# Output products of a cross attention by a Strassen scheme with sums in place, and three quarters of their weights loaded twice

## The chip, the cores and the metric

The kernel runs on one core of a Trainium2 chip. The metric is the device time of one execution in microseconds. Of three runs of the kernel before, the median is 2770.35 us (2768.77 to 2773.72).

## The reference, cut to what matters

One layer of a hybrid decoder serves a prompt of 1024 tokens and 64 sample tokens (8 sequences of 8), with a model width of 1024, in float32. This case is about the second of its three residual blocks, the cross attention:

```python
def cross_attn(xn, mem_kv, w_xq, w_xo):
    q = (xn @ w_xq).reshape(B, S, N_XHEADS, XHEAD_DIM)        # 4 heads of 256
    s = jnp.einsum('bqhd,bkhd->bhqk', q, mem_kv[:, :, 0]) * (XHEAD_DIM ** -0.5)
    p = jax.nn.softmax(s, axis=-1)                            # over 256 memory rows
    o = jnp.einsum('bhqk,bkhd->bqhd', p, mem_kv[:, :, 1])
    return o.reshape(B, S, D_MODEL) @ w_xo
...
xp = xp + cross_attn(rmsnorm(xp, g_xattn[l]), mkv, w_xq[l], w_xo[l])
ff, cb = conv_ffn(rmsnorm(xp, g_ffn[l]), ...)
```

The prompt attends to one memory, each of the 8 sample sequences to a cached one of its own. The product with `w_xo` is 1024 x 1024 x 1024 for the prompt and 64 x 1024 x 1024 for the samples.

## The kernel before, in words

Activations stand transposed (128 channels on the partitions, k = 0 to 7 blocks of channels). A matmul takes 128 tokens of one block k as the stationary side and 512 columns of the weights as the moving side. The residual rows `x_res` stay in SBUF, nine tiles: eight of 128 prompt tokens (t = 0 to 7) and one of the 64 samples (t = 8, `NQ`). A float32 matmul stands in the profile as two records on PE.

**The order of work** is written by `weave`. Each stage is a generator on each engine and yields the planned time of its next piece; `weave` always takes the piece with the earliest planned time. Planned times (table `PLAN`, at its end) only sort the instructions of an engine; at this place a planned 1872 stands at about 1751 us of the trace. An engine executes its list in order, and whatever waits holds all that is behind it. Five parts meet around this change:

- **c**, the output products. `onto_x_pe` (L1934 to L1959) runs them for t = 0 to 7 and h = 0, 1 (halves of the output columns): 8 matmuls (L1948) into bank h, 16 units in all, then the samples, 16 matmuls (L1956) that come last. `crossout_dve` adds each unit onto `x_res` from PSUM (L2371, 512 columns an add). Unit u waits until unit u - 2 has been added. Planned 1848 to 2040. `mix_pe`, `mix_sums` and `mix_dve` (L2034 to L2102) are an earlier stage, the output product of the mixer. It has the seven products of the scheme already, 28 prompt units of 4 matmuls (L2049) with four PSUM banks, and the sums of 128x2048 elements (L2062 to L2087).
- **x**, the prompt's attention (`attention`, L651): 16 units x, of which scores are PE L702, the turned probabilities PE L729, the products with the values PE L718, and the copy of these ("taken") DVE L788.
- **xp**, the samples' attention into the cached memories (`paged`, L1212), one batch b = 0 to 7 after the other: four turns of the keys (T, PE L1287; the copies behind them on ACT L1353 and DVE L1346 in turn), scores (S, PE L1303), their copy and maximum (DVE L1378, L1379, L1388), exponential (ACT L1358), turned probabilities (P, PE L1312; copy DVE L1398), product with the values (V, PE L1323; scaled by DVE L1405), and the turn back (O, PE L1330; copies DVE L1409). It begins on each engine with a wait for the last taken unit of x, and has 72 pieces, spread evenly over its planned time (1872 to 2012). The samples' output products wait for its end.
- **n3**, the norm before the MLP, row tile by row tile: square and root on ACT (L325, L328, with an activation table of its own), reciprocal and scaling on DVE (L348, L354), two groups of four turns on PE (L369), and behind each a multiplying copy on DVE (L340). The scaled row has one buffer and the turned one bank. In the planned time of tile i, of length d, the square stands at 0, the scaling at 0.2 d, the turns at 0.5 d and 0.7 d, the copies at 0.6 d and 0.8 d. A tile's planned time was 20.7 us.
- **sums and first products of the MLP**: `token_sums` (DVE L2588 to L2592, three sums a tile, for tiles 4 to 6 between the others, for 7 and 8 behind them), `weight_sums`, and `first_products_pe` (PE L2518), then the turns of the old rows (PE L2474).

SP issues the loads (`cross_sp`, the cached memories L2294 and L2305, the MLP's weights L2465) and `spill_sp` (L2443), which writes finished rows out.

Of the kernel before, what the change touches and what calls it, by code (L numbers as in the profile page):

```python
# [22 lines left out]
P = 128  # L23
# [29 lines left out]
def rows_of(t):  # L53
    return P if t < NQ else SM
# [47 lines left out]
def make_sample_tables():  # L102
# [46 lines left out]
    memkv=(1577, 1636), q=(1650, 1814), x=(1692, 1856), c=(1848, 2040), n3=(1880, 2066), xp=(1872, 2012))  # L149


def at(stage):
# [20 lines left out]
def build(nc, I, O, TAB):  # L173

    with ExitStack() as ctx:
# [1754 lines left out]
        def onto_x(pfx):  # L1930
            s, z = again("onto_x", "w_in0 w_in1 computed added", lambda n: 2 * TT if n in ("computed", "added") else 16)
            return dict(s=s, z=z)

        def onto_x_pe(pe, a, lhs, w, now, ready):  # L1934

            for t in range(NQ):
                for h in range(2):
                    u = 2 * t + h
                    for k in range(KD):
                        yield now((t + 0.5 * h + 0.5 * k / KD) / (NQ + 0.5))  # L1940
                        if k == 0:
                            if h == 0:
                                ready(pe, t)
                            if t == 0:
                                pe.wait_ge(*nth(a, f"w_in{h}", 16))
                            if u >= 2:
                                pe.wait_ge(*nth(a, "added", u - 1))
                        last = pe.matmul(banks[h], lhs(k)[:, t * P:(t + 1) * P], w[h][:, k, :], start=(k == 0), stop=(k == KD - 1))  # L1948
                    last.then_inc(a["s"]["computed"], 1)
            for k in range(KD):  # L1950
                yield now((NQ + 0.5 * k / KD) / (NQ + 0.5))
                if k == 0:
                    ready(pe, NQ)
                    pe.wait_ge(*nth(a, "added", 2 * NQ - 1))
                for h in range(2):
                    last = pe.matmul(banks[0][h * SM:(h + 1) * SM, :], lhs(k)[:, S:TOK], w[h][:, k, :], start=(k == 0),  # L1956
                                     stop=(k == KD - 1))
                    if k == KD - 1:
                        last.then_inc(a["s"]["computed"], 1)  # L1959

        def onto_x_out(t, h):

            return banks[h] if t < NQ else banks[0][h * SM:(h + 1) * SM, :]

        def onto_x_at(t, h):

            return (t + 0.5 * h + 0.5) / (NQ + 0.5) if t < NQ else 1.0 + 0.01 * h
# [170 lines left out]
        xo = onto_x("crossout")  # L2138

        def cross_unit_due(u):  # L2140

# [205 lines left out]
        def xpages_pe(pe):  # L2347
# [2 lines left out]
            yield from pages_pe(pe, pg_x, lambda e, b, i: landed(e, xk_in[b % 2], b // 2 + 1),  # L2350
                                lambda e, b, i: landed(e, xv_in[b % 2], b // 2 + 1))

        def crossout_pe(pe):
            def ready(eng, t):
                if t == 0:
                    eng.wait_ge(cx["copied"], 32)
                if t < NQ:
                    eng.wait_ge(*nth(att_x, "taken", 12 + t // 2 + 1))
                else:
                    pages_over(eng, pg_x)  # L2360
            yield from onto_x_pe(pe, xo, lambda k: oTc[:, k, :], wX, at("c"), ready)

        def crossout_dve(dve):
            now = at("c")
            for t in range(TT):
                r = rows_of(t)
                for h in range(2):
                    yield now(onto_x_at(t, h))
                    dve.wait_ge(*nth(xo, "computed", 2 * t + h + 1))
                    xr = x_res[0:r, t, 512 * h:512 * h + 512]  # L2370
                    dve.tensor_tensor(xr, xr, onto_x_out(t, h), ALU.add).then_inc(xo["s"]["added"], 1)  # L2371


        NH = 14
# [14 lines left out]
        old_rows = take(2 * FF, B2)  # L2389

        def crossout_ready(eng, i):
            eng.wait_ge(*nth(xo, "added", 2 * (i + 1)))

        n3 = norm(all_tiles, lambda i: x_res[0:rows_of(i), i, :], "g_ffn", xnT, 2 * TT + 2,
                  lambda i: take(D, f0 + 15360), 1, take(D, f0 + 10240), banks[2:3], at("n3"), crossout_ready)
        NF2 = 2 * NF
        NU2 = NF2
        NPR = 14
# [39 lines left out]

        def spill_sp(sp):
            for t in range(TT):  # L2440
                yield at("c")((t + 1) / (NQ + 0.5)) + 1
                sp.wait_ge(*nth(xo, "added", 2 * (t + 1)))
                sp.dma_start(rows_out(t), x_res[0:rows_of(t), t, :]).then_inc(s_xrow[group_of_row[t]][0], 16)  # L2443

        def spilled(eng, groups):
# [4 lines left out]
            eng.wait_ge(s_xrow[i][0], s_xrow[i][1] + 32 * len(ROWS_MOVED[i]))  # L2450

        def mlp_sp(sp):
            yield PLAN["xp"][1] + 10
            pages_over(sp, pg_x)
            sp.dma_start(old_rows[0:16, :], I["cache_ffn_conv"][0].rearrange("b i c -> (b i) c")).then_inc(old_in[0], 16)
            for j in range(NF):
                if j == 1:
                    yield PLAN["n3"][1] + 5
                    sp.wait_ge(*nth(n3, "rooted", TT))
                    spilled(sp, WU_ROWS)  # L2460
                if j >= 2:
                    sp.wait_ge(mp["product"], NPR * (j - 1))
                for a in range(2):
                    i, c = 2 * (j % 2) + a, (j + a * NF) * P
                    sp.dma_start(wu[i], w_up[:, :, c:c + P]).then_inc(wu_in[i][0], 16)  # L2465

        def old_rows_pe(pe):
            landed(pe, old_in, 1)
            pe.wait_ge(*nth(xo, "added", 2 * TT))
# [68 lines left out]
        def mlp_act(act):  # L2538
# [8 lines left out]
            act.wait_ge(*nth(xo, "computed", 2 * TT))  # L2547
# [22 lines left out]
        def sums_dve(dve):  # L2570

            for t in range(4, 7):
                yield at("n3")((t + 1.9) / TT)
                dve.wait_ge(*nth(n3, "kept", 2 * (t + 2)))
                token_sums(dve, t)
            yield at("n3")(8.3 / TT)
            weight_sums(dve, 0)
            yield at("n3")(8.35 / TT)
            fourth_sum(dve, 0)

        def token_sums(dve, t):
# [34 lines left out]
        def mlp_dve(dve):  # L2616
# [35 lines left out]
            dve.wait_ge(*nth(xo, "computed", 2 * TT))  # L2652
# [388 lines left out]
        @block.sync  # L3041
        def _(sp):
            start_sp(sp)
            ptab_sp(sp)
            weave(lf_sp(sp), in_turn(*(dilproj_sp(sp, g) for g in range(NG))), gates_sp(sp),
                  foxprep_sp(sp), foxk_sp(sp), dilprep_sp(sp), dilk_sp(sp), dilv_sp(sp),
                  mix_sp(sp), cross_sp(sp), xpages_sp(sp), xvalues_sp(sp), mlp_sp(sp), spill_sp(sp))
            down_sp(sp)

        @block.gpsimd  # L3050
# [81 lines left out]
```

## Time and profile before

| | |
|---|---|
| median of 3 runs | 2770.35 us |
| the profiled execution: its time | 2772.53 us |
| its span | 2770.7 us |
| PE (TensorE matmul) busy | 2728.6 us, 98% |
| DVE (VectorE) busy | 1151.3 us, 42% |
| ACT (ScalarE) busy | 528.3 us, 19% |
| mean granted clock of TensorE | 0.993 |

PE is the matmul engine, PEld its weight loads, DVE VectorE, ACT ScalarE, SPq the DMA queue of SyncE. The chain of waits is followed back from the last instruction. A timeline row gives start and length in us, engine, line, operation, and in brackets how long the engine was idle before it and what ended that. A windows row gives for a stretch the busy us (and instructions) of PE, PEld, DVE, ACT and POOL, then the granted clock (1.00 is 2.4 GHz, 0.50 is 1.2 GHz), the DMA share and GB/s.

### The profile page before, as it was taken

The page shows a single profiled execution, that of the slowest core. Times are in us where ns is not written, and L with a number is a line of the kernel's source. Part 1 is how long each engine was busy: PE and PEld are TensorE (multiplying, and loading weights), DVE is VectorE, ACT ScalarE, POOL GpSimd, SP SyncE. Part 2 cuts the span into 40 slices and gives each one's busy share as a digit, 9 for nine tenths or more (in the row PEclk, how much of TensorE's full clock was granted, in tenths as well). Part 3 has the DMA queues.
Part 4 walks back from the last instruction along what each step waited for, and adds up shares of the span by engine and source line. Part 5 has one row for each costly group of instructions (what it writes and reads, how often), then busy time and mean ns, then how long its engine had stood idle before and what let it go on. Part 6 is the DMA issues. An engine that isn't in the chain of part 4 may idle for free.

```text
span 2770.7 us, 37655 instructions
## 1 busy us (share of the span) xinstructions
PE 2728.6 (98%) x14274; PEld 1857.1 (67%) x14274; DVE 1151.3 (42%) x2788; ACT 528.3 (19%) x1160; POOL 145.4 (5%) x268
## 2 busy tenths in 40 slices
PE   8999999999999999999999999999999999999998
PEld 7655556767655555456644577546888888888887
DVE  2255543332253233333264023345666666654432
ACT  2233323221201112111002112221112112210002
POOL 1000001020101112100000000000000000000000
PEclk9999999999999999999899999999999999999999
DMA  5000102000116778865511400333445433152201
GB/s 189 22 13 9 59 24 65 28 19 20 44 27 198 214 212 262 244 202 171 200 66 61 152 31 31 130 130 115 140 128 172 149 118 125 46 170 91 82 29 65
DMA packets 207160, 294.48 MB, mean 106 GB/s; under 512 B 20781, under 2 KB 145086, under 8 KB 205942
## 3 DMA queue, kind: packets, MB, share of 16 engines
q1 hardware_dynamic: 148150, 187.76, 20.9%
q10 hardware_dynamic: 42976, 89.26, 10.1%
q0 software_dynamic: 15856, 15.07, 2.2%
q8 instruction: 115, 1.88, 0.3%
q14 instruction: 63, 0.52, 0.1%
HBM read 268.07 MB, written 63.35 MB: 120 GB/s over the span
## 4 chain that ended last, share of the span: by engine, by line
PE 96%; DMA 2%; DVE 1%; issue 1%; ACT 0%; SPq 0%; ACTq 0%; DVEq 0%
PE psum L2518 20%; PE psum L955 11%; PE psum L2898 10%; PE psum L1864 9%; PE psum L531 5%; PE psum L2202 4%; PE psum L1948 4%; PE psum L2049 3%; PE psum L702 3%; PE psum L1287 3%; PE psum L718 3%; PE psum L1872 3%; PE psum L1323 3%; PE psum L1303 2%; PE psum L2176 2%; PE psum L729 2%
## 5 line engine op out<-in xcount | busy, mean ns | idle before, releaser
L2518 PE MATMUL psum<-arena 128*128 128x272 f32 x2464 | 567.3, 394 | 0.5 <-DVE arena L2592 0.5
L2518 PEld LDWEIGHTS psum<-arena 128*128 128x128 f32 x2464 | 470.2, 191 | 97.0 <-issue 0.6
L955 PE MATMUL psum<-arena 128*128 128x512 f32 (+3 forms) x960 | 316.9, 481 | 1.4 <-ACT arena L584 1.4
L1864 PE MATMUL psum<-arena 128*128 128x368 f32 (+1 forms) x768 | 298.2, 489 | 1.4 <-DVE arena L1807 1.2
L2898 PE MATMUL psum<-arena 128*128 128x256 f32 (+1 forms) x1584 | 288.1, 356 | 0.0
L2898 PEld LDWEIGHTS psum<-arena 128*128 128x128 f32 (+1 forms) x1584 | 252.8, 178 | 34.3 <-issue 3.2
L955 PEld LDWEIGHTS psum<-arena 128*128 128x128 f32 (+1 forms) x960 | 195.1, 250 | 62.3 <-issue 35.1
L778 DVE CUSTOM_DVE_ANT_0 arena<-psum,arena 128x256 f32<-128x256 f32 (+2 forms) x224 | 95.4, 457 | 207.0 <-PE psum L702 206.6
L1864 PEld LDWEIGHTS psum<-arena 128*128 128x128 f32 x768 | 123.2, 190 | 68.2 <-issue 42.1
L2621 DVE TENSOR_TENSOR arena<-arena,psum 128x272 f32<-128x272 f32 (+2 forms) x330 | 111.7, 377 | 112.8 <-PE psum L2518 112.0
L752 ACT ACTIVATE arena<-arena 128x256 f32<-128x256 f32 (+4 forms) x192 | 107.5, 562 | 228.7 <-DVE arena L778 227.2
L1287 PEld LDWEIGHTS psum<-arena 128*128 128x128 f32 x848 | 102.1, 141 | 66.4 <-issue 42.1
L1346 DVE COPY arena<-psum 128x512 f32<-128x512 f32 (+1 forms) x108 | 73.6, 682 | 166.2 <-PE psum L1287 166.2
L531 PE MATMUL psum<-arena 128*128 128x288 f32 (+1 forms) x384 | 137.6, 483 | 0.0
L1353 ACT ACTIVATE arena<-psum 128x512 f32<-128x512 f32 (+1 forms) x108 | 63.6, 589 | 377.8 <-PE psum L1287 357.3
L2642 DVE SCALAR_TENSOR_TENSOR arena<-arena 128x1024 f32<-128x1024 f32 x88 | 113.1, 1285 | 52.6 <-ACT arena L2544 51.1
L1287 PE MATMUL psum<-arena 128*128 128x128 f32 x848 | 130.2, 276 | 3.9 <-DMA arena<-in_cache_fox_kv 3.7
L2542 ACT ACTIVATE arena<-arena 128x1024 f32<-128x1024 f32 x44 | 54.2, 1233 | 400.7 <-DVE arena L2621 400.7
L1948 PE MATMUL psum<-arena 128*128 128x512 f32 x256 | 123.5, 599 | 0.0
L2202 PE MATMUL psum<-arena 128*128 128x288 f32 (+1 forms) x384 | 122.6, 468 | 0.0
L3001 DVE TENSOR_TENSOR arena<-arena,psum 128x256 f32<-128x256 f32 (+1 forms) x128 | 46.6, 401 | 178.9 <-PE psum L2898 178.8
L788 DVE COPY arena<-psum 128x128 f32<-128x128 f32 (+1 forms) x96 | 37.6, 391 | 193.4 <-PE psum L718 193.2
(242 smaller groups left out, 2973.7 us busy)
## 6 DMA issues: line engine op xcount, KB each, us to landing
arena<-in_cache_fox_kv ACTq DMA_DIRECT2D x128, 256.0 KB, 4.3
arena<-in_cache_fox_kv SPq DMA_DIRECT2D x128, 256.0 KB, 4.4
out_win_s<-in_cache_win_kv ACTq DMA_DIRECT2D x8, 4080.0 KB, 15.4
arena<-in_w_up SPq DMA_DIRECT2D x44, 512.0 KB, 6.3
arena<-in_w_down SPq DMA_DIRECT2D x14, 1408.0 KB, 6.3
arena<-in_cache_win_kv SPq DMA_DIRECT2D x16, 1024.0 KB, 7.9
arena<-in_cache_mem_kv SPq DMA_DIRECT2D x16, 1024.0 KB, 6.3
arena<-in_w_in SPq DMA_DIRECT2D x9, 1024.0 KB, 7.8
```

The lines of the kernel that those rows point to most:

```text
L531: last = pe.matmul(banks[q % 2][:, 0:cw], w[:, k, j * P:(j + 1) * P], xnT[:, k, c0:c0 + cw], start=(k == 0), stop=(k == KD - 1))
L752: act.activation(p, p, ACT.Exp, scale=-1.0, bias=a["NM"][i], accum_out=a["L"][i]).then_inc(s["expd"], 1)
L778: dve.tensor_tensor_reduce(a["Pb"][i % 4][:, c0:c1], SCORE[h][:, 0:c1 - c0], un["add"](h)[:, c0:c1], 1.0, a["GM"][:, i % 4:i % 4 + 1] if c ...
L955: last = pe.matmul(banks[c0 // 512][p0:p0 + r, 0:n], xn_tile(k, g, t), wD[g][:, k, w0:w0 + n], start=(k == 0), stop=(k == KD - 1))
L1287: last = pe.transpose(a["turn"][n % 2][:, x * P:(x + 1) * P], k, ident)
L1864: last = pe.matmul(banks[0][:, 0:cw], w[:, k, :], xnT[:, k, c0:c0 + cw], start=(k == 0), stop=(k == KD - 1))
L1948: last = pe.matmul(banks[h], lhs(k)[:, t * P:(t + 1) * P], w[h][:, k, :], start=(k == 0), stop=(k == KD - 1))
L2202: last = pe.matmul(banks[u % 2][:, 0:cw], wX[n % 2][:, k, (m % 4) * P:(m % 4 + 1) * P], xnT[:, k, c0:c0 + cw], start=(k == 0), stop=(k == ...
L2518: last = pe.matmul(bank_of(j, x, p), w[:, k, :], r[:, k, Q4 * p:Q4 * p + Q4], start=(k == 0), stop=(k == 3))
L2621: last = dve.tensor_tensor(dst, dst if base is None else view(base), view(bank), ALU.add)
L2642: dve.scalar_tensor_tensor(out=tp, in0=up[:, tap:tap + S], scalar=w, in1=tp, op0=ALU.mult, op1=ALU.add).then_inc(done, 1)
L2898: last = pe.matmul(down_out(u)[p0:p0 + r, 0:n], hT(f)[:, tok + t * P:tok + t * P + r], slot[slots[c]][:, f - fa, c0:c0 + n], start=(f == f ...
```

## The change

The prompt's output products are cut into quarters (512 tokens, 512 channels, 512 columns) and computed by seven products in place of eight. There are 28 units of 4 matmuls in two banks, four for each product, then the samples' unit of 16 matmuls. The quarter sums are formed in place: four over the attention's output, four over the weights. For the samples, whose output needs the plain weights, three quarters of `w_xo` are loaded again, each when its last reader is done. Rows 0 to 3 of `x_res` are now complete with product p6 and rows 4 to 7 with p4, the last. The planned times of c, xp and n3 are new, and so is the point where the samples' products stand (2032).

```diff
-    ... c=(1848, 2040), n3=(1880, 2066), xp=(1872, 2012))
+    ... c=(1844, 2004), n3=(1972, 2066), xp=(1872, 2024))
-            yield from onto_x_pe(pe, xo, lambda k: oTc[:, k, :], wX, at("c"), ready)
+        C_UNITS = [(name, t) for name in ("p1", "p2", "p7", "p5", "p3", "p6", "p4") for t in range(4)] + [("s", NQ)]
+        N_CU = len(C_UNITS)
+        def cross_at(u):
+            return at("c")(u / 28) if u < 28 else 2032 + 10 * (u - 28)
+        def cross_over(u):
+            return at("c")((u + 1) / 28) if u < 28 else 2042
+        def n3_at(x):
+            return 1972 + 5.7 * 9 * x if 9 * x < 8 else 2043 + 23 * (9 * x - 8)
+        def cross_again_sp(sp):
+            yield cross_over(c_done("p7") - 1) + 1
+            sp.wait_ge(*nth(xo, "computed", c_done("p7")))
+            sp.dma_start(wX[1][:, 0:4, :], w_xo[:, 0:4, 512:1024]).then_inc(xo["s"]["w_in1"], 16)
+            yield cross_over(c_done("p6") - 1) + 1
+            sp.wait_ge(*nth(xo, "computed", c_done("p6")))
+            sp.wait_ge(*nth(cw, "summed", 4))
+            sp.dma_start(wX[0][:, 0:4, :], w_xo[:, 0:4, 0:512]).then_inc(xo["s"]["w_in0"], 16)
+            yield cross_over(c_done("p4") - 1) + 1
+            sp.wait_ge(*nth(xo, "computed", c_done("p4")))
+            sp.dma_start(wX[0][:, 4:8, :], w_xo[:, 4:8, 0:512]).then_inc(xo["s"]["w_in0"], 16)
+        def cross_operands_ready(pe, name):
...
+            elif name == "p7":
+                pe.wait_ge(*nth(cw, "summed", 2))
+                pe.wait_ge(*nth(ch, "summed", 1))
...
+            else:
+                pages_over(pe, pg_x)
+                pe.wait_ge(*nth(xo, "w_in1", 32))
+                pe.wait_ge(*nth(xo, "w_in0", 48))
         def crossout_pe(pe):
+            for u, (name, t) in enumerate(C_UNITS):
+                yield cross_at(u)
+                if t == 0 or name == "s":
+                    cross_operands_ready(pe, name)
+                if u >= 2:
+                    pe.wait_ge(*nth(xo, "added", u - 1))
...
+                    for k in range(4):
+                        if k:
+                            yield cross_at(u + k / 4)
+                        last = pe.matmul(banks[u % 2], oTc[:, ks, tok + t * P:tok + (t + 1) * P][:, k, :], wX[side][:, ws, :][:, k, :],
+                                         start=(k == 0), stop=(k == 3))
+                last.then_inc(xo["s"]["computed"], 1)
+        def cross_sums(dve, name, t):
+            if (name, t) == ("p2", 0):
+                dve.wait_ge(*nth(xo, "computed", c_done("p1")))
+                dve.wait_ge(*nth(att_x, "taken", 8))
+                dve.tensor_tensor(part(M_LOW, 0), part(M_LOW, 0), part(M_LOW, 512), ALU.subtract).then_inc(ch["s"]["summed"], 1)
+                dve.wait_ge(*nth(xo, "w_in0", 16))
+                dve.wait_ge(*nth(xo, "w_in1", 16))
+                dve.tensor_tensor(b11, b12, b11, ALU.subtract).then_inc(cw["s"]["summed"], 1)
+            elif (name, t) == ("p2", 1):
...
         def crossout_dve(dve):
+            for u, (name, t) in enumerate(C_UNITS):
+                yield cross_over(u)
+                dve.wait_ge(*nth(xo, "computed", u + 1))
+                for half, side in M_ONTO.get(name, ((2, 0), (2, 1))):
...
+                    last = dve.tensor_tensor(xr, xr, src, ALU.add)
+                last.then_inc(xo["s"]["added"], 1)
+                cross_sums(dve, name, t)
+        def cross_row_done(i):
+            return N_CU if i == NQ else c_done("p6", i) if i < 4 else c_done("p4", i - 4)
 def spill_sp(sp):
-                yield at("c")((t + 1) / (NQ + 0.5)) + 1
+                yield cross_over(cross_row_done(t) - 1) + 2
 def mlp_sp(sp):
-            yield PLAN["xp"][1] + 10
+            yield PLAN["xp"][1] + 4
 def first_products_pe(pe):
-                    yield at("c")(1.02) + 0.1 * (2 * x + p)
+                    yield 2043.8 + 0.1 * (2 * x + p)
 def sums_dve(dve):
-                yield at("n3")((t + 1.9) / TT)
+                yield n3_at((t + 1.9) / TT)
```

The other sums follow the pattern shown: one behind the adds of (p2, 1), (p7, 0), (p5, 0), (p5, 1), (p3, 0) and (p3, 1). An add of a unit of p1 has four parts (one for each quarter of the output), p2, p3 and p4 one, p7 and p5 two, p6 three. The three reloads are of 1 MB each.

## Rows read from the trace of the kernel before

**Rows 1.** The page: busy time of the engines, and the chain's shares

```profile
PE 2728.6 (98%) x14274; PEld 1857.1 (67%) x14274; DVE 1151.3 (42%) x2788; ACT 528.3 (19%) x1160; POOL 145.4 (5%) x268
PE 96%; DMA 2%; DVE 1%; issue 1%; ACT 0%; SPq 0%; ACTq 0%; DVEq 0%
```

**Rows 2.** Window over most of the stage

```profile
1752.00:1877.00 125.00, 125.00 (x658) 61.36 (x657) 48.49 (x120) 40.58 (x66) 0.00 (x0) 1.00 0.42 148
```

**Rows 3.** Groups by line, 1729 to 1910 us: busy, mean ns, idle before

```profile
L1948 PE MATMUL psum<-arena 128*128 128x512 f32 x256 | 123.5, 599 | 0.0
L2371 DVE TENSOR_TENSOR arena<-arena,psum 128x512 f32<-128x512 f32 (+1 forms) x18 | 12.3, 684 | 16.3 <-PE psum L1948 14.2 <-PE psum L1956 2.0
```

**Rows 4.** Timeline of DVE in the mixer's output product

```profile
1411.56 2.28 DVE L2062 TENSOR_TENSOR arena<-arena 128x2048 f32<-128x2048 f32 x1
1413.76 2.29 DVE L2066 TENSOR_TENSOR arena<-arena 128x2048 f32<-128x2048 f32 x1
...
1469.32 1.89 DVE L2099 SCALAR_TENSOR_TENSOR arena<-psum,arena 128x512 f32<-128x512 f32 x3 [1.55 <-PE psum L2049]
...
1472.75 1.89 DVE L2099 SCALAR_TENSOR_TENSOR arena<-psum,arena 128x512 f32<-128x512 f32 x3 [0.69 <-PE psum L2049]
```

**Rows 5.** Timeline of PE where the prompt's attention ends

```profile
1750.52 1.02 PE L1948 MATMUL psum<-arena 128*128 128x512 f32 x2
1751.67 0.63 PE L1287 MATMUL psum<-arena 128*128 128x128 f32 x4
```

**Rows 6.** Timeline of ACT: an exponential, then a row of the norm

```profile
1775.88 0.51 ACT L1358 ACTIVATE arena<-arena 128x256 f32<-128x256 f32 x1 [2.25 <-DVE arena L1388]
...
1776.38 1.04 ACT L325 ACTIVATE arena<-arena 128x1024 f32<-128x1024 f32 x1
...
1777.54 1.28 ACT L328 ACT_TABLE_LOAD   x1
1778.83 0.29 ACT L328 ACTIVATE arena<-arena 128x1 f32<-128x1 f32 x1
```

**Rows 7.** Timeline of DVE, 1859 to 1885 us

```profile
1865.05 0.48 DVE L1405 TENSOR_SCALAR arena<-psum,arena 128x256 f32<-128x256 f32 x1 [2.37 <-issue]
...
1868.76 0.42 DVE L1378 COPY arena<-psum 128x256 f32<-128x256 f32 x1 [0.58 <-PE psum L1303]
...
1869.43 0.55 DVE L2588 TENSOR_TENSOR arena<-arena 128x384 f32<-128x384 f32 x1
...
1876.29 0.75 DVE L354 TENSOR_SCALAR arena<-arena 128x1024 f32<-128x1024 f32 x1
...
1882.81 0.69 DVE L340 TENSOR_TENSOR arena<-psum,arena 128x512 f32<-128x512 f32 x1 [0.61 <-PE psum L369]
1883.53 0.69 DVE L2588 TENSOR_TENSOR arena<-arena 128x512 f32<-128x512 f32 x1
```

**Rows 8.** Timeline of PE, 1866 to 1910 us

```profile
1866.69 1.02 PE L1948 MATMUL psum<-arena 128*128 128x512 f32 x2
1867.64 1.05 PE L1303 MATMUL psum<-arena 128*8 128x256 f32 x16
1868.63 2.84 PE L1948 MATMUL psum<-arena 128*128 128x512 f32 x6
...
1876.36 0.38 PE L1330 MATMUL psum<-arena 128*128 128x128 f32 x2
...
1888.71 4.51 PE L1956 MATMUL psum<-arena 128*64 128x512 f32 x20
...
1909.87 20.36 PE L2518 MATMUL psum<-arena 128*128 128x272 f32 x78 [0.54 <-DVE arena L2592]
```

**Rows 9.** Where the clock fell: a row of PE's timeline, two windows

```profile
1397.45 1.09 PE L369 MATMUL psum<-arena 128*128 128x128 f32 x8 [2.43 <-DVE arena L354]
1366.00:1370.00 4.00, 4.00 (x21) 4.00 (x20) 0.00 (x0) 0.00 (x0) 0.00 (x0) 0.50 1.05 395
1400.00:1404.00 4.00, 4.00 (x14) 1.10 (x12) 0.30 (x1) 0.00 (x0) 0.00 (x0) 0.70 0.00 0
```

More of the change, by code:

```diff
@@ L1927, in gates_dve @@
             dve.tensor_tensor(merged[:, :, S:TOK], sgs[:, 0, :, :], sgs[:, 1, :, :], ALU.add).then_inc(gt["s_merged"], 1)
[L1930 to L1967, printed above, removed]
         wm = [take(4096, f0 + 4096 * i).rearrange("p (k n) -> p k n", k=KD) for i in range(2)]
@@ L2351, in xpages_pe @@
                                 lambda e, b, i: landed(e, xv_in[b % 2], b // 2 + 1))
-        def crossout_pe(pe):
[L2354 to L2358, printed above, removed]
-                else:
-                    pages_over(eng, pg_x)
-            yield from onto_x_pe(pe, xo, lambda k: oTc[:, k, :], wX, at("c"), ready)
-        def crossout_dve(dve):
[L2364 to L2371, printed above, removed]
+        def cross_operands_ready(pe, name):
+            if name == "p1":
+                pe.wait_ge(cx["copied"], 32)
+                pe.wait_ge(*nth(att_x, "taken", 8))
+                pe.wait_ge(*nth(xo, "w_in0", 16))
+            elif name == "p2":
+                pe.wait_ge(*nth(att_x, "taken", 14))
+            elif name == "p7":
+                pe.wait_ge(*nth(cw, "summed", 2))
+                pe.wait_ge(*nth(ch, "summed", 1))
+            elif name == "p5":
+                pe.wait_ge(*nth(ch, "summed", 2))
+            elif name == "p3":
+                pe.wait_ge(*nth(ch, "summed", 4))
+            elif name == "p6":
+                pe.wait_ge(*nth(cw, "summed", 3))
+            elif name == "p4":
+                pe.wait_ge(*nth(cw, "summed", 4))
+            else:
+                pages_over(pe, pg_x)
+                pe.wait_ge(*nth(xo, "w_in1", 32))
+                pe.wait_ge(*nth(xo, "w_in0", 48))
@@ new lines, in crossout_pe @@
+        def crossout_pe(pe):
+            for u, (name, t) in enumerate(C_UNITS):
[4 more added lines that the diff above has]
+                    pe.wait_ge(*nth(xo, "added", u - 1))
+                if name == "s":
+                    for k in range(KD):
+                        if k:
+                            yield cross_at(u + k / KD)
+                        for h in range(2):
+                            last = pe.matmul(banks[u % 2][h * SM:(h + 1) * SM, :], oTc[:, k, S:TOK], wX[h][:, k, :],
+                                             start=(k == 0), stop=(k == KD - 1))
+                else:
+                    ks, tok, side, ws = M_WHERE[name]
+                    for k in range(4):
+                        if k:
+                            yield cross_at(u + k / 4)
+                        last = pe.matmul(banks[u % 2], oTc[:, ks, tok + t * P:tok + (t + 1) * P][:, k, :], wX[side][:, ws, :][:, k, :],
+                                         start=(k == 0), stop=(k == 3))
+                last.then_inc(xo["s"]["computed"], 1)
@@ new lines, in cross_sums, with part @@
+        def cross_sums(dve, name, t):
+            def part(ks, tok):
+                return oTc[:, ks, tok:tok + 512]
+            b11, b21, b12, b22 = wX[0][:, M_LOW, :], wX[0][:, M_HIGH, :], wX[1][:, M_LOW, :], wX[1][:, M_HIGH, :]
+            if (name, t) == ("p2", 0):
[6 more added lines that the diff above has]
+            elif (name, t) == ("p2", 1):
+                dve.wait_ge(*nth(cw, "summed", 1))
+                dve.tensor_tensor(b12, b22, b12, ALU.subtract).then_inc(cw["s"]["summed"], 1)
+            elif (name, t) == ("p7", 0):
+                dve.wait_ge(*nth(ch, "summed", 1))
+                dve.wait_ge(*nth(att_x, "taken", 16))
+                dve.tensor_tensor(part(M_LOW, 512), part(M_LOW, 512), part(M_HIGH, 512), ALU.add).then_inc(ch["s"]["summed"], 1)
+            elif (name, t) == ("p5", 0):
+                dve.wait_ge(*nth(xo, "computed", c_done("p7")))
+                dve.wait_ge(*nth(ch, "summed", 2))
+                dve.tensor_tensor(part(M_LOW, 0), part(M_HIGH, 512), part(M_LOW, 0), ALU.subtract).then_inc(ch["s"]["summed"], 1)
+            elif (name, t) == ("p5", 1):
+                dve.wait_ge(*nth(xo, "computed", c_done("p2")))
+                dve.wait_ge(*nth(ch, "summed", 3))
+                dve.tensor_tensor(part(M_HIGH, 0), part(M_HIGH, 0), part(M_LOW, 0), ALU.subtract).then_inc(ch["s"]["summed"], 1)
+            elif (name, t) == ("p3", 0):
+                dve.wait_ge(*nth(xo, "computed", c_done("p5")))
+                dve.wait_ge(*nth(cw, "summed", 2))
+                dve.tensor_tensor(b11, b22, b11, ALU.subtract).then_inc(cw["s"]["summed"], 1)
+            elif (name, t) == ("p3", 1):
+                dve.wait_ge(*nth(cw, "summed", 3))
+                dve.tensor_tensor(b21, b21, b11, ALU.subtract).then_inc(cw["s"]["summed"], 1)
@@ new lines, in crossout_dve @@
+        def crossout_dve(dve):
+            for u, (name, t) in enumerate(C_UNITS):
+                yield cross_over(u)
+                dve.wait_ge(*nth(xo, "computed", u + 1))
+                for half, side in M_ONTO.get(name, ((2, 0), (2, 1))):
+                    tile_, r = (4 * half + t, P) if half < 2 else (NQ, SM)
+                    xr = x_res[0:r, tile_, 512 * side:512 * side + 512]
+                    src = banks[u % 2] if half < 2 else banks[u % 2][side * SM:(side + 1) * SM, :]
+                    last = dve.tensor_tensor(xr, xr, src, ALU.add)
+                last.then_inc(xo["s"]["added"], 1)
+                cross_sums(dve, name, t)
@@ L2391, in crossout_ready @@
         def crossout_ready(eng, i):
-            eng.wait_ge(*nth(xo, "added", 2 * (i + 1)))
+            eng.wait_ge(*nth(xo, "added", cross_row_done(i)))
         n3 = norm(all_tiles, lambda i: x_res[0:rows_of(i), i, :], "g_ffn", xnT, 2 * TT + 2,
-                  lambda i: take(D, f0 + 15360), 1, take(D, f0 + 10240), banks[2:3], at("n3"), crossout_ready)
+                  lambda i: take(D, f0 + 15360), 1, take(D, f0 + 10240), banks[2:3], n3_at, crossout_ready)
         NF2 = 2 * NF
@@ L2440, in spill_sp @@
             for t in range(TT):
-                yield at("c")((t + 1) / (NQ + 0.5)) + 1
-                sp.wait_ge(*nth(xo, "added", 2 * (t + 1)))
+                yield cross_over(cross_row_done(t) - 1) + 2
+                sp.wait_ge(*nth(xo, "added", cross_row_done(t)))
                 sp.dma_start(rows_out(t), x_res[0:rows_of(t), t, :]).then_inc(s_xrow[group_of_row[t]][0], 16)
@@ L2468, in old_rows_pe @@
             landed(pe, old_in, 1)
-            pe.wait_ge(*nth(xo, "added", 2 * TT))
+            pe.wait_ge(*nth(xo, "added", N_CU))
             for q in range(2):
@@ L2651, in mlp_dve @@
             dve.wait_ge(mp["old_turned"], 1)
-            dve.wait_ge(*nth(xo, "computed", 2 * TT))
+            dve.wait_ge(*nth(xo, "computed", N_CU))
             dve.wait_ge(*nth(n3, "turned", 2 * TT))
```

18 lines of the change are left out of this document (12 added, 6 removed).

## The prediction

> **What bounds the kernel now.** I read the page first: PE is busy for 98% of the span and carries 96% of the chain that ended last [rows 1]. The reader should see that a microsecond taken from PE's list is gained only while PE stays fed. The window over the stage says it is: 125.00 of 125 us busy, with DVE at 39% and ACT at 32% [rows 2]. The groups by line give the size: the prompt's output products are 256 records with no idle time before them [rows 3]. The timelines then show what holds the stage so full. The prompt's attention hands over to the samples' pages with no gap worth naming [rows 5], and single matmuls of the output product stand between all small pieces of the pages [rows 8]. They are the filler that hides every chain through DVE and ACT. The last page piece starts at 1876.36, and 12 us of products still follow before the samples' unit at 1888.71 [rows 8].
>
> **What is removed.** In the mixer's stage, a prompt unit of four matmuls takes 1472.75 - 1469.32 = 3.43 us, 0.86 a matmul [rows 4]. Eight products become seven: 128 matmuls become 112, so PE's list is shorter by 16 x 0.86 = **13.7 us**. The samples' unit is the same.
>
> **What is added off PE.** DVE gets 56 adds for 16, 40 x 0.6 = 24 us (three in a row take 1.89 [rows 4]), and eight sums of 2.2 = 18 us [rows 4]. In a stage of some 165 us it goes from about 39% to about 65%: no bound by its total. With two banks a unit's adds must be over before the second next unit starts, 3.4 us later and more: the longest, four adds, take 2.5 and fit. I cost the bank ring at nothing; if DVE comes late once, it is under 1 us. The three reloads are issued by SP with 0.4 us each. Two have tens of microseconds, the last has all of the tail below (21 us); an 8 us landing is covered by it. They would show only if the tail went.
>
> **What the new order exposes.** I wrote out the lists of PE, DVE and ACT from the planned times and went through them with the durations of the rows. An instruction starts when its engine is free and what it waits for is done, plus 0.05 us. The same working on the old order ends at 1909.9 us, where the trace has 1909.87 [rows 8].
>
> *Where the pages begin: 4.2 us.* The add of (p2, 0) is planned at 1872.57 and the last taken unit at 1872.91, so DVE does the add and two sums first: 0.6 + 2.2 + 2.2, then 0.7 for the copy, 5.8 us after the unit's last matmul. PE has only the 1.7 us of that attention unit's product with the values, and then the first turn of the pages, which waits for the copy. Before, two records of the output product stood there and hid it [rows 5]. 5.8 + 0.2 - 1.7 gives 4.2.
>
> *Row 1 of the norm: 3.2 us.* A norm row now has 5.7 planned us, its first turn 2.85 after its square. On ACT the square of row 1 stands behind the exponential of batch 5. From the start of that batch's scores on PE: scores 1.2, until DVE has done three other adds, the copy, the maximum and a keep 3.2, exponential 0.6, square to root 2.7 with the table load [rows 6], reciprocal and scaling 0.95 [rows 7], 7.6 in all. PE has scores, a turn, three matmuls and O, 4.4 us. Other small stops of the stretch come to 1.6 us.
>
> *The tail: 13.3 us.* The products are planned to end at 2004, the pages at 2024. Behind the last product PE has P and V of batch 6, two turns, S, P, V and O of batch 7, O of 6, and the turns of norm rows 5, 6 and 7: 2 x 0.22, 2 x 0.44, 3 x 1.2 (1.05 and the gaps beside it [rows 8]), 2 x 0.22 and 6 x 0.44, 7.9 us, and no matmul between them. DVE has to do between them three groups of token sums (1.8, 2.2 and 2.2 us: three of 0.55, then of 0.69 [rows 7]), two scalings with reciprocal (0.95), six copies of 0.6 to 0.7, and the pages' copies. In order, PE idles 0.95 us for the copy between the turns of row 5; 2.4 for row 6's scaling, behind the token sums of tile 4; 1.6 for its copy, behind a key copy; 3.5 for row 7's scaling, behind the token sums of tile 5 and the scores' copy of 0.67 [rows 7]; 0.7 for its copy; 3.2 for batch 7's V, whose P copy stands behind the token sums of tile 6; 0.55 for O behind the scaling of 0.48 [rows 7]; 0.55 for the samples' unit. Sum 13.35. What follows that unit (first products, row 8) is as before.
>
> *The clock.* After an idle of 2.43 us among turns the granted clock fell for part of the next window (0.70 over 4 us), and in a stretch of stops and narrow products it stayed at 0.50, 1.2 GHz [rows 9]. The new tail is such a stretch. Nothing shows how long it lasts here. Lower end: 0. Upper end: from 8 us into the tail to the middle of the first products, with PE's pieces on the path twice as long, 7.6, and a spell of 3.4 us costing 1.7 at each of the two stalls ahead, 11 in all. I take 4.1, one spell over the tail's last two thirds and the samples' first half, nearest to the row of 0.50.
>
> Sum: -13.7 + 4.2 + 3.2 + 1.6 + 13.3 - 0.2 (stops of the old order that go) = **+8.4**, with the clock +12.5. The profiled execution, 2772.53 us (span 2770.7), would become 2785; on the median, 2.2 below it, **2783 us**. What a measurement of this kernel can tell from no change is about 0.2%, 5.5 us.
>
> **A rule against the change.** The Trainium skill (TensorE: Matmul & The Clock Gate, "A second HAM failure mode") says that frequent short idles between groups of matmuls, without one long gap, are enough for the clock to swing between half and full. Here row and rule agree in direction [rows 9]; by the rule the upper end of the clock's cost would be the one to take. The sums above do not need it.
>
> **Rivals.**
> 1. *The clock stays down from the first stalls through the samples' unit and the first products.* For it: the 0.50 window above. Against it: the stretch up to the tail is dense. 8.4 + 11 = +19.4, 2790 us.
> 2. *The stalls are half of what I count*, because a wait is met earlier on ACT or DVE (rooted rows ahead, copies overlapping). Then 11 of 22 us stay and the clock holds: -13.7 + 11 + 2 = about -1 to +5, 2769 to 2775, same.
> 3. *The other side: faster.* One mechanism: PE is fed in the tail after all, because the pages' chain and the norm are done by the time the products end. It decides where the last product's end and the end of batch 7 meet. If PE idles there under 3 us and only the 4.2 at the pages' start stays, -13.7 + 4.2 + 3 = -6.5, down to -12 with both gone: 2758 to 2764. For it: before, pages and norm never made PE wait in this stage [rows 2]. Against it: planned 20 us of pages stand behind the last product, and PE's list has no filler there. With the tail gone the last reload would show too.
> 4. *The change doesn't do what it says*: a reload lands so late that the samples' unit waits for it. It would take over 21 us; together with a DVE that falls behind the two banks, above 2793.
>
> **How the numbers follow.** My forecast (2777 to 2787) has 0.52, rival 1 0.18, rival 2 0.16, rival 3 0.10, rival 4 0.04. The range leaves out rivals 3 and 4 and the bottom of rival 2: 2771 to 2793. Same is 2764.8 to 2775.9: rival 2 nearly whole, 0.15. Faster: rival 3, 0.10. Slower: the rest, 0.75.
>
> **What the profile would show.** Right: L1948's groups replaced by 224 records; PE idle of about 4 us released by DVE's taken copy where the pages begin; one of about 3 us before a turn of the norm, released by the scaling; a window of some 21 us before the samples' unit with PE busy for 8 to 12; clock under 1.00 there; the MLP after it unchanged but later. Wrong: that window full, or idle time before the prompt units released by their adds, or by a DMA at the samples' unit. PE's busy time should fall by 10 to 13 us while the span grows.

## The result, and the profile after

The changed kernel takes 2788.48 us (median of 4 runs, 2785.87 to 2791.83) against 2771.81 us of the kernel before (4 runs; the 2770.35 above is the median of the first three): ratio 1.006, 95% interval 1.0042 to 1.0079. It is slower by 16.7 us. The profiled execution took 2786.17 us with a span of 2784.4, so its own difference is 13.7 us of span.

The page of the changed kernel, the lines that answer to [rows 1]:

```profile
PE 2719.7 (98%) x14242; PEld 1845.9 (66%) x14242; DVE 1192.8 (43%) x2836; ACT 520.4 (19%) x1154; POOL 145.4 (5%) x268
PE 94%; DMA 2%; DVE 2%; issue 1%; ACT 0%; ACTq 0%; SPq 0%; DVEq 0%
```

PE is busy for 8.9 us less and the span is 13.7 us longer. DVE is busy for 41.5 us more. PE's share of the chain falls from 96% to 94%. The groups by line over the stage, 1729 to 1925 us, answer to [rows 3]. L2392 are now the prompt's output products, L2385 the samples', and L2440 their adds on DVE:

```profile
L2392 PE MATMUL psum<-arena 128*128 128x512 f32 x220 | 109.1, 612 | 0.0
L2440 DVE TENSOR_TENSOR arena<-arena,psum 128x512 f32<-128x512 f32 (+1 forms) x58 | 37.2, 681 | 19.7 <-PE psum L2392 9.8 <-PE psum L2385 9.8
L369 PE MATMUL psum<-arena 128*128 128x128 f32 (+1 forms) x72 | 12.9, 308 | 11.8 <-DVE arena L354 8.8 <-DVE arena L340 3.0
```

The prompt's products never wait (0.0), so the two banks and their adds cost nothing. The costliest waits are those before the norm's turns, 11.8 us. Timeline rows of PE that have an idle time before them, from the pages' start to the samples' unit:

```profile
1754.56 1.09 PE L1287 MATMUL psum<-arena 128*128 128x128 f32 x4 [4.26 <-DVE arena L788]
...
1852.84 1.11 PE L369 MATMUL psum<-arena 128*128 128x128 f32 x4 [2.94 <-DVE arena L354]
...
1866.71 0.66 PE L369 MATMUL psum<-arena 128*128 128x128 f32 x4 [0.78 <-DVE arena L354]
...
1879.31 0.66 PE L369 MATMUL psum<-arena 128*128 128x128 f32 x4 [0.79 <-DVE arena L340]
...
1883.78 0.65 PE L369 MATMUL psum<-arena 128*128 128x128 f32 x4 [2.40 <-DVE arena L354]
...
1886.25 0.98 PE L369 MATMUL psum<-arena 128*128 128x128 f32 x4 [1.38 <-DVE arena L340]
...
1891.71 1.11 PE L369 MATMUL psum<-arena 128*128 128x128 f32 x4 [2.66 <-DVE arena L354]
...
1893.61 1.11 PE L369 MATMUL psum<-arena 128*128 128x128 f32 x4 [0.36 <-DVE arena L340]
...
1897.93 1.89 PE L1323 MATMUL psum<-arena 128*8 128x256 f32 x16 [2.78 <-issue]
...
1900.48 0.69 PE L1330 MATMUL psum<-arena 128*128 128x128 f32 x2 [0.66 <-DVE arena L1405]
...
1901.56 9.73 PE L2385 MATMUL psum<-arena 128*64 128x512 f32 x32 [0.38 <-DVE arena L1409]
```

They sum to 19.4 us. In the kernel before this stretch has no idle row of this kind [rows 2]. The lengths show the clock as well: four turns take 0.66 us at full clock and 1.11 at half, the samples' unit 9.73 us where it took 7.3 in the kernel before. Windows of the changed kernel (busy us of PE, PEld, DVE, ACT, POOL, then granted clock, DMA share, GB/s), before, in and behind the waits:

```profile
1753.00:1757.00 4.00, 2.44 (x6) 1.58 (x7) 1.30 (x2) 0.60 (x1) 0.00 (x0) 0.54 0.34 81
1757.00:1761.00 4.00, 4.00 (x11) 2.11 (x10) 0.69 (x1) 0.00 (x0) 0.00 (x0) 0.61 0.98 358
1765.00:1850.00 85.00, 84.77 (x424) 39.32 (x422) 49.17 (x93) 14.79 (x29) 0.00 (x0) 1.00 0.47 164
1853.00:1857.00 4.00, 4.00 (x16) 2.57 (x17) 2.82 (x5) 0.17 (x1) 0.00 (x0) 0.66 0.41 156
1886.00:1907.00 21.00, 13.91 (x64) 5.78 (x66) 9.14 (x22) 0.60 (x2) 0.00 (x0) 0.51 0.24 38
```

Between the two places PE is full (84.77 of 85 us). At each of the three places the clock falls to 1.2 GHz, and from 1886 to 1907 us it is at 0.51.

**A length that leaves the rest out.** Single runs of one kernel differ by up to 19 us (22 runs of the kernel before: 2762.64 to 2781.82), and the stretch before this stage alone moved by up to 19 us between traces. So the experiments are also read by one length inside the trace: from the start of the first product with `w_xq` to the start of the last product with `w_up`. Everything the change touches lies in it. The views by line of the kernel before and of the changed one (min, median and max ns; first and last start in us):

```profile
L2202 PE MATMUL psum<-arena x384: 405/407/595, 1555.8 to 1715.4; 128*128 128x288 f32 x128, 128*128 128x512 f32 x64
L2518 PE MATMUL psum<-arena x2464: 392/393/792, 1897.0 to 2469.3; 128*128 128x272 f32 x190
```

```profile
L2198 PE MATMUL psum<-arena x384: 406/406/595, 1552.8 to 1712.4; 128*128 128x288 f32 x128, 128*128 128x512 f32 x64
L2593 PE MATMUL psum<-arena x2464: 392/392/792, 1911.2 to 2483.0; 128*128 128x272 f32 x190
```

Before: 2469.3 - 1555.8 = 913.5 us. After: 930.2 us, **16.7 us** more, which is the difference of the medians too. The stretch ahead, which the change does not touch, was 3 us shorter in this trace; in another trace of the same order of work (e4 below) it is 4 us longer.

### The profile page after: what moved, and what is told of

Read it like the earlier page. It is cut to its first block, busy times and chain, and to the rows that moved or that the text cites. A ratio compares the mean times of both kernels' runs of the same rounds, so it can differ in the third digit from the quotient of the medians.

```text
span 2784.4 us, 37643 instructions
## 1 busy us (share of the span) xinstructions
PE 2719.7 (98%) x14242; PEld 1845.9 (66%) x14242; DVE 1192.8 (43%) x2836; ACT 520.4 (19%) x1154; POOL 145.4 (5%) x268
## 4 chain that ended last, share of the span: by engine, by line
PE 94%; DMA 2%; DVE 2%; issue 1%; ACT 0%; ACTq 0%; SPq 0%; DVEq 0%
PE psum L2593 20%; PE psum L955 11%; PE psum L2973 10%; PE psum L1864 9%; PE psum L531 5%; PE psum L2198 4%; PE psum L1287 3%; PE psum L702 3%; PE psum L2392 3%; PE psum L1872 3%; PE psum L718 3%; PE psum L2010 3%; PE psum L1323 2%; PE psum L1303 2%; PE psum L2172 2%; PE psum L729 2%
## 5 line engine op out<-in xcount | busy, mean ns | idle before, releaser
L788 DVE COPY arena<-psum 128x128 f32<-128x128 f32 (+1 forms) x96 | 37.5, 391 | 184.8 <-PE psum L718 184.6
L2392 PE MATMUL psum<-arena 128*128 128x512 f32 x224 | 110.9, 612 | 0.0
```

What stands on the lines that cost most here:

```text
L2392: last = pe.matmul(banks[u % 2], oTc[:, ks, tok + t * P:tok + (t + 1) * P][:, k, :], wX[side][:, ws, :][:, k, :], start=(k == 0), stop=(k ...
```

## The experiments

Theory: PE's list is 13.7 us shorter, and the new order opens waits at three places where nothing fills PE, in which the clock falls. Rivals: the pages or the norm bound the stage anyway; DVE's added work; the reloads; or only waits and no clock. Eight experiments were made. The times of e1 to e4 are set against 22 runs of the kernel before (median 2769.09 us), those of e5 to e8 against 35 (2772.80).

A stage length is that of one execution. To each belong two more figures, taken over the same stretch of the same trace: the time in which PE is idle, and the time in which PE is busy while the granted clock is at 0.50. The last column adds up three terms against the kernel before: the list of PE (-13.8 us, as e2 measures it; e3 adds the 15.4 us of its fillers), the difference in idle time, and half of the difference in busy time at 0.50. The half is an estimate: it takes the work to be twice as long at half clock.

| run | stage length, us | against before | ratio of times to before, 95% interval | PE idle, us | PE busy at 0.50, us | sum of the three terms |
|---|---|---|---|---|---|---|
| before | 913.5 | | | 1.7 | 6.3 |  |
| changed | 930.2 | +16.7 | 1.006 (1.0042 to 1.0079) | 21.8 | 25.3 | +15.8 |
| e1_changed_again | 930.2 | +16.7 | 1.0052 (1.0033 to 1.0072) | 21.8 | 25.4 | +15.9 |
| e2_before_112 | 899.7 | -13.8 | 0.9962 (0.9945 to 0.9979) | 1.7 | 6.3 | -13.8 |
| e3_filled_stalls | 922.5 | +9.0 | 1.0031 (1.0017 to 1.0044) | 8.4 | 5.9 | +8.1 |
| e4_small_reloads | 931.8 | +18.3 | 1.0072 (1.005 to 1.0095) | 21.8 | 29.0 | +17.7 |
| e5_sums_later | 923.4 | +9.9 | 1.0031 (1.0016 to 1.0045) | 18.6 | 17.9 | +8.9 |
| e6_token_sums_later | 928.4 | +14.9 | 1.0039 (1.0022 to 1.0056) | 18.4 | 28.8 | +14.2 |
| e7_pages_earlier | 921.8 | +8.3 | 1.0017 (1.0006 to 1.0029) | 16.7 | 16.6 | +6.4 |
| e8_all_reordered | 903.8 | -9.7 | 0.9972 (0.9958 to 0.9986) | 5.9 | 3.3 | -11.1 |

The sum comes within 2 us of every length, so PE's list, its idle time and the half clock are nearly all that the runs differ by. By the whole times e3, e5 and e6 are not told apart from the changed kernel (their intervals overlap that of e1); what they show rests on the lengths and the traces.

**The changed kernel once more.**

> The changed kernel once more, beside the kernel before, for the size of the loss and its spread. My theory (stalls of PE at three places where its list has no filler, and the clock that falls in them): 12 to 18 us slower, ratio 1.0045 to 1.0065. If the loss shown so far were a matter of which runs were taken (rival: no change), under 5 us.

Measured: 14.8 us slower (2783.91 against 2769.09), stage length 930.2 again, with the waits of 4.26, 2.94, 2.40, 2.67 and 2.78 us in the same places. The waits are set by the order, not by chance.

**The shorter list alone, in the old order.**

```diff
 def onto_x_pe(...)
-                    for k in range(KD):
+                    for k in range(KD - 1):
...
-                                    start=(k == 0), stop=(k == KD - 1))
+                                    start=(k == 0), stop=(k == KD - 2))
```

> The kernel before with the last of the eight channel blocks left out of the prompt's output products: 112 matmuls in place of 128, as in the scheme, and nothing else moved. This is the shorter list of PE alone. Theory: every microsecond less on PE is gained while PE stays fed, so 13.7 us faster, ratio 0.995; PE idle time in the stage under 3 us. Rival: the pages or the norm are the true bound of the stage and hold the end where it was: under 5 us gained, and PE idles before turns.

Measured: the length is 13.8 us shorter, the time 7.7 us by the medians, 10.5 by the ratio. This kernel leaves out one block of channels, so its result is wrong. The windows of this kernel over the stage:

```profile
1752.00:1862.00 110.00, 109.87 (x581) 55.98 (x579) 42.68 (x105) 37.86 (x61) 0.00 (x0) 1.00 0.47 163
1862.00:1890.00 28.00, 28.00 (x136) 12.06 (x136) 12.95 (x29) 4.77 (x9) 0.00 (x0) 1.00 0.37 88
```

PE stays fed with 112 matmuls in the old order. The rival (pages or norm as the true bound) falls: 16 matmuls less are worth their 0.86 us each.

**Idle time filled with matmuls that nobody reads.**

```diff
+        def filler_pe(pe):
+            for due, n, b, done in ((1871.95, 8, 1, 4), (1980.5, 6, 0, 23), (2009.0, 5, 0, 27), (2010.1, 2, 0, 27),
+                                    (2014.7, 6, 0, 27), (2019.7, 6, 0, 27)):
+                yield due
+                pe.wait_ge(*nth(xo, "added", done))
+                for _ in range(n):
+                    pe.matmul(banks[b][:, 0:256], ident, cst["band_mask"], start=True, stop=True)
```

> The changed kernel with 33 matmuls of 128x256 that nobody reads put into PE's list just before the places where it waits (8 where the pages begin, 6 before the first turn of norm row 1, 19 in the tail): some 14 us of idle time filled, and none of the waits changed. If the clock is a part of the loss, as the 0.50 windows say, the granted clock of the tail rises to 1.00 and the time falls by 3 to 8 us against the changed kernel. If only the waits count (rival), the time stays or grows by up to 3 us, since some fillers are longer than what is left of a wait.

Measured: the length falls by 7.7 us against the changed kernel, at the upper end of what was expected, and the medians by 6.4 (2777.56 against 2783.91). Windows of the filled tail, to be held against 1886 to 1907 above:

```profile
1880.00:1900.00 20.00, 16.72 (x123) 11.29 (x122) 13.92 (x31) 5.14 (x10) 0.00 (x0) 1.00 0.20 76
1900.00:1910.00 10.00, 10.00 (x47) 4.93 (x44) 1.37 (x2) 1.95 (x3) 0.00 (x0) 1.00 0.83 160
```

The clock is at 1.00 in the tail and at both stalls ahead of it, and the samples' unit takes 7.09 us. More work on PE made the stage shorter. The fillers are 15.4 us of work where PE's idle time fell by 13.4, so some 2 us of them outlast the waits. What is left, +9.0, is near the +8.4 that the prediction has for the waits without the clock.

**The second loads without their bytes.**

```diff
-            sp.dma_start(wX[1][:, 0:4, :], w_xo[:, 0:4, 512:1024])...
+            sp.dma_start(wX[1][0:1, 0:4, :], w_xo[0:1, 0:4, 512:1024])...
...
```

(and so for the other two loads)

> The changed kernel with the three second loads of the weights cut from 1 MB to one partition's part of it, so that the samples' products take wrong weights for three quarters. Same number of loads and waits, almost no bytes. Theory: the reloads lie under the tail, so no change against the changed kernel (within 3 us). Rival (the second loads delay the pages' loads, or the samples' unit waits for them): 4 to 10 us faster than the changed kernel.

Measured: nothing gained; the length is 1.6 us longer than that of the changed kernel, with the same waits, and the clock was low for 6.8 us in place of 3.4 both at the second stall and where the MLP begins. The median is 7.3 us above that of e1 (2791.21 against 2783.91), more than the 3 us expected, but the intervals of the two ratios overlap, and of the 7.2 us between the two profiled spans the stage length has only 1.6. In the changed kernel the last reload landed 4.9 us after its issue, some 19 us before the samples' unit began. The rival falls.

**The sums where the pages begin, moved behind the copy.**

```diff
             if (name, t) == ("p2", 0):
+                yield 1873.0
                 dve.wait_ge(*nth(xo, "computed", c_done("p1")))
...
+                yield 1880.0
                 dve.wait_ge(*nth(xo, "w_in0", 16))
...
-                cross_sums(dve, name, t)
+                yield from cross_sums(dve, name, t)
```

> The changed kernel with one thing moved on DVE: the first sum over the attention's output comes at a planned 1873.0, behind the copy of the last taken unit (1872.91), and the first sum over the weights at 1880.0. Theory: PE's wait of 4.26 us where the pages begin shrinks to about 1 us, another of about 1 us appears behind the sums, and the clock does not fall there: 3.6 us of waits and 3.4 us of clock less than the changed kernel, stage from the first q product to the last MLP product near 924 us (930.2 in the changed kernel). Rival: the wait only moves to the next piece that needs DVE, nothing gained (930).

Measured: 6.8 us less length (923.4, 924 expected). DVE's timeline in the changed kernel, then in this one:

```profile
1748.61 0.69 DVE L2440 TENSOR_TENSOR arena<-arena,psum 128x512 f32<-128x512 f32 x1 [0.95 <-PE psum L2392]
1749.22 2.28 DVE L2405 TENSOR_TENSOR arena<-arena 128x2048 f32<-128x2048 f32 x1
1751.42 2.29 DVE L2408 TENSOR_TENSOR arena<-arena 128x2048 f32<-128x2048 f32 x1
1753.62 0.68 DVE L788 COPY arena<-psum 128x512 f32<-128x512 f32 x1
```

```profile
1753.25 0.69 DVE L2442 TENSOR_TENSOR arena<-arena,psum 128x512 f32<-128x512 f32 x1 [0.95 <-PE psum L2392]
1754.97 0.69 DVE L788 COPY arena<-psum 128x512 f32<-128x512 f32 x1 [1.04 <-PE psum L718]
1755.85 2.29 DVE L2406 TENSOR_TENSOR arena<-arena 128x2048 f32<-128x2048 f32 x1 [0.19 <-DVE arena L788]
```

Two sums stood between an add and the copy (L788) that lets the pages begin. With the sums behind it PE waits 0.98 us for 4.26, and the clock holds there. The expected wait of 1 us behind the sums didn't come. In the tail the low clock lasted as long as before (6.8 and 13.7 us in two spells). At row 1 of the norm PE still waits 2.94 us, but here the clock held, which was not expected:

```profile
1849.00:1856.00 7.00, 4.74 (x22) 2.75 (x23) 5.12 (x14) 2.54 (x5) 0.00 (x0) 1.00 0.60 215
```

So the gain is some 3.2 us of waits and some 3.7 us of clock, and the clock's part comes from two places, not from the pages' start alone. Whether moving the sums kept the clock up at row 1 or chance did is not shown.

**The token sums, moved behind the pages.**

```diff
-                yield n3_at((t + 1.9) / TT)
+                yield 2030 + t
```

> The changed kernel with the token sums of tiles 4 to 6 (6.2 us of DVE) moved behind the last piece of the pages. Theory: they stand on DVE in front of what PE waits for in the tail, so the tail's idle time falls from 13.3 to 9 us, and the stage by 4.3 us and up to 2 of clock, to 924 to 926 us. Rival: what PE waits for is the chain of the pages itself, not DVE's queue, and the sums were in its gaps: under 1.5 us gained.

Measured: 1.8 us less, where 4.3 to 6 were expected. The three waits of the tail did shrink, from 2.40, 2.66 and 2.78 to 2.06, 1.74 and 0.59 us, 3.5 together. But this trace has a spell of 6.8 us of low clock at the norm's row 1 where the changed one has 3.4, and 17.1 in the tail and 6.8 at the MLP's start for 20.5 and 3.4. PE is busy at 0.50 for 3.5 us more in all, which costs half of it: 3.4 us less of idle time and 1.7 us more of slower work give the 1.8 us. So the token sums are a part of the tail's waits, and the smaller one.

**The pages, planned to end at 2011.**

```diff
-    ... xp=(1872, 2024))
+    ... xp=(1872, 2011))
```

> The changed kernel with the pages planned to end at 2011 in place of 2024, so that fewer of them stand behind the last product. Theory: the matmuls of p4 stand between them again, 5.9 us of waits less, and with the clock 6 to 12 less: stage 918 to 924 us. PE still waits for the scaling of row 7 (4 us). Rival: DVE, with 13 us less for the same adds, sums and copies, makes PE wait earlier in the stage, before the units or before the pages' pieces: no gain (928 to 932).

Measured: 8.4 us less (921.8, 918 to 924 expected). The wait at row 1 of the norm is gone, that at the end of the pages is 0.80 us, and the wait for row 7's scaling grew to 3.82 us, as expected. DVE did not make PE wait before a unit; one wait of 0.64 us appeared before a page's P.

**Everything reordered.**

```diff
-    ... c=(1844, 2004), n3=(1972, 2066), xp=(1872, 2024))
+    ... c=(1844, 2006), n3=(1972, 2066), xp=(1872, 2011))
...
-            return at("c")(u / 28) if u < 28 else 2032 + 10 * (u - 28)
+            return at("c")(u / 28) if u < 28 else 2014.5 + 10 * (u - 28)
...
-            return 1972 + 5.7 * 9 * x if 9 * x < 8 else 2043 + 23 * (9 * x - 8)
+            i = int(9 * x + 1e-6)
+            return 1972 + 5.7 * i + 7.2 * (9 * x - i) if i < 8 else 2025.5 + 23 * (9 * x - 8)
...
             if (name, t) == ("p2", 0):
+                yield 1877.5
                 dve.wait_ge(*nth(xo, "computed", c_done("p1")))
...
+                yield 1878.0
                 dve.wait_ge(*nth(xo, "w_in0", 16))
...
-                yield n3_at((t + 1.9) / TT)
+                yield 2012 + t
-                    yield 2043.8 + 0.1 * (2 * x + p)
+                    yield 2026.3 + 0.1 * (2 * x + p)
```

(`cross_over` of the samples' unit moves with `cross_at`, from 2042 to 2024.5)

> All three together, and the samples' unit, the first products and the norm's row 8 moved up by 17.5 planned us, with row 7's turns inside the samples' unit; within a norm row the scaling and turns come 26% later behind its square, and c ends at 2006. Theory: the waits fall from 23 to about 6 us and the clock holds outside the end, so that the 13.7 us of products are kept for the most part: stage 903 to 907 us, 7 to 10 us under the kernel before, ratio 0.9965. The last reload is the next thing to wait for (1.6 us). Rival: some wait that the order hid so far (the reload, DVE behind the two banks) takes back what is gained, and the stage ends no better than before (913 us or more).

Measured: 903.8 us, 26.4 less than the changed kernel and 9.7 less than the kernel before; 2765.89 against 2772.80 us, ratio 0.9972 (0.9958 to 0.9986). It beats both, though its gain over the kernel before is 4.1 us short of what the list is worth (13.8); PE is idle for 5.9 us over the stage length, for 1.7 before. Windows over the stage, and the idle rows of its end:

```profile
1752.00:1877.00 125.00, 124.47 (x646) 61.56 (x644) 81.96 (x153) 29.95 (x58) 0.00 (x0) 1.00 0.47 165
1877.00:1885.00 8.00, 5.30 (x40) 2.22 (x38) 6.47 (x15) 1.60 (x4) 0.00 (x0) 1.00 0.91 244
```

```profile
1878.78 0.44 PE L1330 MATMUL psum<-arena 128*128 128x128 f32 x2 [0.67 <-DVE arena L1405]
1879.63 0.66 PE L369 MATMUL psum<-arena 128*128 128x128 f32 x4 [0.42 <-DVE arena L354]
1881.08 0.66 PE L369 MATMUL psum<-arena 128*128 128x128 f32 x4 [0.79 <-DVE arena L340]
1882.56 1.08 PE L2386 MATMUL psum<-arena 128*64 128x512 f32 x4 [0.83 <-DMA arena<-in_w_xo]
```

DVE is at 82 of 125 us there, 66%, and holds PE up once, for 0.40 us before a turn of the norm. The reload is the next wait, as expected, with 0.83 us.

## Why the prediction was right

It said 2783 us, slower with a chance of 0.75. Measured were 2788.5, inside the range (2771 to 2793), 5.5 us above the forecast and 1.5 us above the likeliest case's own range (2777 to 2787). The path was right: the list of PE shorter by what was said, and waits opened at the three places named. Two terms were off in opposite directions. The waits came to 20.1 us for 22.1, the clock to 10.4 for 4.1; that the first error took a third of the second back is luck.

- *The term removed*: 13.7 us forecast, 13.8 measured alone (e2).
- *Where the pages begin*: 4.2 us forecast, 4.26 in the trace, released by DVE's L788. e5 shows the two sums as the cause. The terms written there give 4.3 (5.8 + 0.2 - 1.7), not 4.2.
- *Row 1 of the norm*: 3.2 forecast, 2.94 in the trace. The *other small stops* ahead of the tail came to 0.78 us for 1.6.
- *The tail*: the eight waits were forecast as 0.95, 2.4, 1.6, 3.5, 0.7, 3.2, 0.55, 0.55. They came as 0.79, 2.40, 1.38, 2.66, 0.36, 2.78, 0.66, 0.38: 11.4 us for 13.45, as the eight terms add up (13.35 is a slip, as is 7.9 for PE's own work there, which adds up to 8.0). The 21 us before the samples' unit, 1880.5 to 1901.5, have PE busy for 10.44, where 8 to 12 were forecast. Part of the difference is PE's own work at half clock, which fills the waits it lies beside (turns of 1.11 us, a V of 1.89). That this is a cause is argued, not shown.
- *DVE's total, the banks and the reloads at nothing*: right. PE waits for no unit's add and for no load, and DVE's busy time grew by 41.5 us where 42 were forecast. PE's busy time fell by 8.9 us and not by 10 to 13, since work at half clock is busy for longer.
- *The clock*: the term that was mis-sized. The prediction took 4.1 us, one spell over two thirds of the tail and half of the samples' unit, and left the two stalls ahead to its upper end. The trace has a spell at each stall (6.8 and 3.4 us) and one of 20.5 us, over the last 15 us of the tail and the first half of the samples' unit. What the waits leave of the 16.7 is this: PE is idle for 21.8 us over the stage length and for 1.7 before, so 16.7 + 13.8 - 20.1 = 10.4 us are slower work, near the prediction's upper end of 11. Two other readings agree. Half of the busy time at 0.50, 25.3 us against 6.3 before, is 9.5 us. And e3, in which no spell is left ahead of the MLP, gives back 7.7 us although some 2 us of its fillers outlast the waits. The kernel before has a spell of its own where the MLP begins (6.8 us, 3.4 in the changed kernel), which the prediction did not count. For its row of 0.50 the prediction speaks of stops and narrow products; PE was busy for 4.00 of 4 us in that row [rows 9], so it is a row of narrow work rather than of stops.

The first rival had more of this mechanism than the forecast, with 2790 us for its price, and the measured time lies nearer to it. But its "stays down from the first stalls" is not what happened: between the stalls and the tail the clock was at 1.00, for 85 us from 1765 to 1850, and only 3.4 us of the first products ran at half.

The Trainium skill's rule that frequent short idles let the clock swing (TensorE: Matmul & The Clock Gate, "A second HAM failure mode") spoke for that rival. The Trainium skill tells it there of another kernel, in bf16. This trace agrees that no long wait is needed: 0.51 over 1886 to 1907 us, with no idle over 2.8 us in it. It differs in that the clock did not swing there but stayed at half for 20.5 us. The rival on the other side, that PE would be fed in the tail, fell with the rows above; the order of e8 makes it true, at its price (-9.7 us, -6.5 to -12 there).

What stays open is what decides whether a spell comes and how long it lasts. The two traces of the changed kernel had the same spells in this stage; e4, with the same order and the same waits, had 6.8 us for 3.4 at two places; and e5 had none after the same 2.94 us at row 1. One spell more or less of 3.4 us moves a stage length by up to 1.7 us, so differences of that size between the lengths are not read as effects. The 1.9 us by which the sum for e7 misses its length, and the 1.4 for e8, are not explained.

## What to carry to other kernels

A product scheme that saves matmuls on an engine that is always busy also takes away filler: look at what the removed or moved matmuls stood between, and at when each output is complete, since here all rows came due at the end and their norms and the pages' chain were left with nothing between them. Write out the in-order lists of the engines at each place where one stage hands over to the next; here that gave each wait to within a microsecond, and a long operation that is not urgent in front of a short one that is (two sums of 2.3 us ahead of a copy) cost 4.3 us of waiting, and the stage was 6.8 us shorter without it. Price an idle stretch of TensorE with its clock: here 20 us of waits brought some 10 us of slower work. To compare orders of work, take three figures from each trace over the same stretch: PE's list, its idle time, and its busy time at half clock.

## What the runs showed of the hardware that was not expected

In the changed kernel the clock fell at the waits of 4.26 and 2.94 us and stayed at half for 6.8 and 3.4 us, for the most part while PE was already full again (0.61 over 1757 to 1761 us, PE busy for 4.00 of 4). The wait alone does not settle it: after the same 2.94 us before the same turn of the norm the spell lasted 3.4 us in two traces and 6.8 in two others (e4, e6), and in e5 there was none (1.00 over 1849 to 1856 us). Thirty-three matmuls that nobody reads, 15.4 us of work, shortened the stage by 7.7 us. Outside this stage the same kernel is less steady than thought: about where the mixer's output product begins (1347 to 1387 us) a spell of half clock lasted 3.4 us in the two traces of the changed kernel and 20.5 to 23.9 in seven others, and e6 had none; and the stage's start moved from 1546 to 1565 us between traces, more than this change is worth.
